# Low parts of the feed-forward halves on VectorE alone, the second norm's weights multiplied in by GpSimd along the rows, turned rows copied out of PSUM by ScalarE

## The reference, cut to what matters

```python
x = x + mix.astype(x.dtype) @ w_out
y, conv_new = _conv_ffn(_rmsnorm(x, norm2), conv_st, w_g, w_u, conv_w, conv_b, w_d)
x = x + y
# _rmsnorm(x, g) = x * rsqrt(mean(x*x) + EPS) * g, over the 1024 columns of a row
# _conv_ffn: g = h @ w_g; u = h @ w_u; (gelu(causal dwconv3(g)) * u) @ w_d, with 2816 inner columns
```

## Time and profile before

| | |
|---|---|
| median of 3 runs | 1403.74 us |
| profiled execution | 1402.94 us, of which span 1401.1 us |
| TensorE busy | 1362.7 us, 97% of the span |
| VectorE, ScalarE, GpSimd busy | 55%, 34%, 39% of the span |
| chain that ended last | TensorE 91% |
| mean granted clock of TensorE | 0.992 |

### The profile page before, as it was taken

One profiled execution on the slowest core, in us unless ns is written; L12 is line 12 of the kernel. 1 busy time (PEld: TensorE's weight loads), 2 busy tenths in 40 slices (PEclk: granted clock), 3 DMA queues, 4 the chain that ended last, 5 costly groups with the idle time before them and its releaser, 6 DMA issues.

```text
span 1401.1 us, 23239 instructions
## 1 busy us (share of the span) xinstructions
PE 1362.7 (97%) x9267; PEld 1235.9 (88%) x9267; DVE 774.9 (55%) x1394; ACT 472.3 (34%) x970; POOL 539.7 (39%) x503
## 2 busy tenths in 40 slices
PE   7999999999999999979999999999999999999997
PEld 6988888889998788879999999999999878888886
DVE  4544131557642455788666666667666676333335
ACT  5341242333332244654333333333333351120212
POOL 5130342457642344684444434344444261120200
PEclk9999999999999999989999999999999999999999
DMA  6222632344427675111212122121212671130203
GB/s 244 72 81 83 214 117 80 106 154 148 132 77 260 235 232 175 68 67 48 94 58 85 59 84 80 62 95 57 86 57 85 225 284 64 64 128 19 110 15 120
DMA packets 81754, 158.56 MB, mean 113 GB/s; under 512 B 6967, under 2 KB 42579, under 8 KB 81135
## 3 DMA queue, kind: packets, MB, share of 16 engines
q1 hardware_dynamic: 81503, 157.01, 32.4%
q10 hardware_dynamic: 144, 0.07, 0.0%
HBM read 110.71 MB, written 46.34 MB: 112 GB/s over the span
## 4 chain that ended last, share of the span: by engine, by line
PE 91%; DVE 3%; POOL 2%; DMA 1%; ACT 1%; issue 1%; SPq 0%; DVEq 0%; ACTq 0%; POOLq 0%
PE bank L93 17%; PE bank L95 16%; PE bank L94 16%; PE bank L110 11%; PE bank L111 11%; PE bank L112 11%; PE bank L2029 1%; PE bank L1222 1%; PE bank L1279 1%; PE bank L1982 1%; DMA m_t_in<-scratch_pT 1%; PE bank L1297 1%; PE bank L2012 0%; PE bank L2041 0%; DMA p_arena<-in_x 0%
## 5 line engine op out<-in xcount | busy, mean ns | idle before, releaser
L303 POOL TENSOR_TENSOR w_lo<-w_raw,w_hi 128x512 fp32r<-128x512 f32 x75 | 106.1, 1429 | 154.6 <-ACT w_hi L298 154.6
L2742 DVE TENSOR_TENSOR d_x<-bank,d_x 128x512 f32<-128x512 f32 x126 | 85.5, 689 | 139.9 <-PE bank L95 139.8
L927 POOL TENSOR_TENSOR w_lo<-w_raw,w_hi 128x1024 fp32r<-128x1024 f32 x33 | 79.1, 2409 | 132.7 <-ACT w_hi L1004 132.5
L110 PE MATMUL bank<-f_t_hi,w_hi 128*128 128x256 f32 (+1 forms) x412 | 121.9, 296 | 0.0
L111 PE MATMUL bank<-f_t_lo,w_hi 128*128 128x256 f32 (+1 forms) x412 | 121.6, 295 | 0.0
L112 PE MATMUL bank<-f_t_hi,w_lo 128*128 128x256 f32 (+1 forms) x412 | 121.5, 295 | 0.0
L93 PE MATMUL bank<-w_hi,p_h1T_hi 128*128 128x512 f32 x288 | 113.0, 392 | 1.0 <-POOL w_lo L927 1.0
L93 PE MATMUL bank<-w_hi,d_a_hi 128*128 128x512 f32 x288 | 113.7, 395 | 0.0
L94 PE MATMUL bank<-w_lo,d_a_hi 128*128 128x512 f32 x288 | 113.7, 395 | 0.0
L95 PE MATMUL bank<-w_hi,d_a_lo 128*128 128x512 f32 x288 | 113.6, 395 | 0.0
L110 PE MATMUL bank<-f_b_hi,w_hi 128*128 128x320 f32 (+1 forms) x360 | 108.3, 301 | 4.3 <-DVE f_gate_prompt L2481 3.6
(11 more groups left out here) (326 smaller groups left out, 3644.5 us busy)
## 6 DMA issues: line engine op xcount, KB each, us to landing
w_raw<-in_w SPq DMA_DIRECT2D x81, 512.0 KB, 4.7
e_a_lo<-scratch_act SPq DMA_DIRECT2D x22, 576.0 KB, 7.1
scratch_pN<-p_n_out SPq DMA_DIRECT2D x36, 256.0 KB, 2.1
c_lo<-in_w SPq DMA_DIRECT2D x16, 512.0 KB, 6.4
scratch_act<-c_hi SPq DMA_DIRECT2D x22, 320.0 KB, 2.1
scratch_pT<-p_t_out SPq DMA_DIRECT2D x36, 192.0 KB, 1.9
scratch_act<-c_lo SPq DMA_DIRECT2D x22, 256.0 KB, 2.0
p_arena<-in_x SPq DMA_DIRECT2D x9, 512.0 KB, 6.0
```

Source lines behind the costliest of these rows:

```text
L110: pe.matmul(out, stat[0], mov[0], start=start, stop=False, skip_group_check=True)
L303: pool.tensor_tensor(lo, self.unit_source(n), hi.bitcast(F32), ALU.subtract).then_inc(self.unit_split, 1)
L927: pool.tensor_tensor(w_lo[:, i % NS_, :], raw[:, i % 2, :], w_hi[:, i % NS_, :].bitcast(F32), ALU.subtract).then_inc(g["piece_split"], 1)
L2742: dve.tensor_tensor(x, bank[DOWN_BANKS[n % 8]], x, ALU.add).then_inc(added.sem, 1)
```

## The change

Three things move, and the hand-written order with them.

1. The weights `norm2` are no longer multiplied in after the turn. GpSimd multiplies each row tile by them before, along the rows (`apply_gain`, new name `("gained", c)` in the order, one 128x1024 operation for each of nine tiles, between `sum` and `scaled`). For that the 1024 weights must lie in every partition: SyncE first copies the column form to a row in DRAM (1024 elements of 4 bytes) and later loads this row into all partitions (`gain`, 512 KB). `scaled` now waits for `gained`.
2. The turned rows are copied out of PSUM by ScalarE (`raw_rows` with ACTIVATE Copy), two 128x512 copies for each tile. Tile 7's copies (`last_rows`) move to ScalarE's program in gate_up.
3. All fourteen low parts of the row operands are made by VectorE, in ScalarE's order of high parts. VectorE's program at the start of gate_up is rewritten for that; GpSimd keeps the low parts of the weights alone.

```diff
+    def apply_gain(self, pool, c):
+        self.gain_in.wait(pool, 32)
+        pool.wait_ge(self.x_loaded[c], 32)
+        pool.tensor_tensor(self.x9[:, c, :], self.x9[:, c, :], self.gain[:, :], ALU.mult).then_inc(self.gained, 1)
+
+    def raw_rows(self, act, bank, c, i):
         p, at = (0, c) if c < 5 else (1, c - 5)
         dst = (self.k1, self.k2)[i][p][:, :, at * P:(at + 1) * P]
-        gain = self.cols[:, K_N2 + i * KH:K_N2 + (i + 1) * KH].unsqueeze(2).to_broadcast([P, KH, P])
-        return dve.tensor_tensor(dst, bank.rearrange("p (k f) -> p k f", k=KH), gain, ALU.mult)
+        return act.activation(dst, bank.rearrange("p (k f) -> p k f", k=KH), ACT.Copy)
...
-        order += {4: [("scaled", 0)], 5: [("scaled", 1)], 6: [("scaled", 2), ("unit", 0)],
-                  7: [("plus", 0), ("plus", 1), ("unit", 1), ("scaled", 3)], 8: [("t", 0, 0)]}.get(s, [])
+        order += {4: [("gained", 0), ("scaled", 0)], 5: [("gained", 1), ("scaled", 1)], 6: [("gained", 2), ("scaled", 2), ("unit", 0)],
+                  7: [("plus", 0), ("plus", 1), ("unit", 1), ("gained", 3), ("scaled", 3)], 8: [("t", 0, 0)]}.get(s, [])
...
         def scale(act, c):
             act.wait_ge(g["norm_root"], M_STEPS.index(c) + 1)
-            act.wait_ge(x_loaded[c], 32)
+            act.wait_ge(half.gained, TURNED.index(c) + 1)
             act.activation(x9[:, c, :], x9[:, c, :], ACT.Copy, scale=rstd2[:, c:c + 1]).then_inc(half.scaled, 1)
...
         load_piece(1)
+        sp.dma_start(row.rearrange("o (k p) -> p (o k)", p=P), a["cols"][:, K_N2:K_N2 + KD],
+                     allow_slow_non_contiguous=True).then_inc(half.gain_in.sem, 16)
...
             elif x[0] == "sum" and x[2] == 1:
+                if x[1] == 1:
+                    sp.wait_ge(g["state_out"], 16)
+                    half.gain_in.wait(sp, 16)
+                    sp.dma_start(half.gain[:, :], row.to_broadcast([P, D])).then_inc(half.gain_in.sem, 16)
...
-        for x in ((1, 0), (1, 1), (0, 5)):
-            half.lo(pool, x)
         done.hidden(pool)
         done.states(pool)
         pool.memset(gp[:, 0:2], 0.0).then_inc(zeroed, 1)
-        half.lo(pool, (1, 4))
-        half.unit_lo(pool, 7)
-        half.unit_lo(pool, 8)
-        half.lo(pool, (1, 5))
-        for n in range(9, 7 * NF):
+        for n in range(7, 7 * NF):
             half.unit_lo(pool, n)
...
+        half.lo(dve, (0, 2))
         half.lo(dve, (0, 3))
         take_up1(0)
         half.lo(dve, (0, 4))
-        last_rows()
-        for k in range(3):
-            half.turned_sum(dve, 1, k)
+        half.lo(dve, (1, 0))
+        half.lo(dve, (1, 1))
         for t in range(QUADS):
             f, p = divmod(t, 2)
             if t != 1:
                 take_c22(t)
             if t == 0:
+                half.lo(dve, (0, 5))
                 half.lo(dve, (0, 6))
+                for k in range(3):
+                    half.turned_sum(dve, 1, k)
                 half.lo(dve, (1, 2))
-                half.turned_sum(dve, 1, 3)
-                half.lo(dve, (1, 3))
...
             take_c21(t)
+            if t == 0:
+                half.lo(dve, (1, 3))
+                half.turned_sum(dve, 1, 3)
+                half.lo(dve, (1, 4))
+                take_up1(1)
+                half.lo(dve, (1, 5))
+                half.lo(dve, (1, 6))
+                take_c22(1)
             conv(t)
```

More of the change, by code:

```diff
@@ L383, in half_split @@
     def half_split(self, x):
-        return (self.half_pool, HALF_POOL.index(x) + 1) if x in HALF_POOL else (self.half_dve, HALF_DVE.index(x) + 1)
+        return self.half_dve, HALF_DVE.index(x) + 1
     def halves_wait(self, eng, p):
-        for order, s in ((HALF_POOL, self.half_pool), (HALF_DVE, self.half_dve)):
-            eng.wait_ge(s, max(i for i, x in enumerate(order) if x[0] == p) + 1)
+        eng.wait_ge(self.half_dve, max(i for i, x in enumerate(HALF_DVE) if x[0] == p) + 1)
     def hi(self, act, x):
@@ L430, in build @@
         res = nc.dram_tensor("scratch_res", (RT, P, D), F32, kind="Internal").ap()
+        row = nc.dram_tensor("scratch_row", (1, D), F32, kind="Internal").ap()
         act_a = nc.dram_tensor("scratch_act", (NF, P, ROWS), F32, kind="Internal").ap()
@@ L438, in build @@
         done = back(nc, a, o, mem_m, early, half, done, const[:, :], cols, col_m, col_d, ssq, ssn, rstd2, power, w, raw, bank,
-                    sem, block)
+                    row, sem, block)
         tiles = DownTiles(a, mem_d, mem_e, w, plain, act_a, old)
@@ L1661, in back_entries @@
         elif x[0] == "turn_n":
-            out += [(x + (i,), "dve") for i in range(2)]
+            out += [(x + (i,), "act") for i in range(2)]
         elif x[0] in ("num", "um"):
@@ L1665, in back_entries, with back @@
     return out
-def back(nc, a, o, mem, early, half, done, ident, cols, col_m, col_d, ssq, ssn, rstd2, power, w, raw, bank, sem, block):
+def back(nc, a, o, mem, early, half, done, ident, cols, col_m, col_d, ssq, ssn, rstd2, power, w, raw, bank, row, sem, block):
     order = back_order()
@@ L1876, in _ @@
                     .then_inc(g["piece_split"], 1)
+            elif name == "gained":
+                half.apply_gain(pool, s)
             elif name == "unit":
                 half.unit_lo(pool, s)
-            elif name == "lo" and x[1:] in HALF_POOL:
-                half.lo(pool, x[1:])
     @block.scalar
@@ L1935, in _ @@
                 Done.scale(act, s)
+            elif name == "turn_n":
+                if s == TURNED[0]:
+                    act.wait_ge(g["state_out"], 16)
+                if s == TURNED[5]:
+                    Done.raw_free(act)
+                for i in range(2):
+                    wait_filled(act, x + (i,))
+                    half.raw_rows(act, ring.bank(x + (i,)), s, i).then_inc(taken["act"], 1)
             elif name == "unit":
@@ L2153, in _ @@
                 clear_state()
-            elif name == "turn_n":
-                if s == TURNED[0]:
-                    dve.wait_ge(g["state_out"], 16)
-                if s == TURNED[5]:
-                    Done.raw_free(dve)
-                for i in range(2):
-                    wait_filled(dve, x + (i,))
-                    u = half.raw_rows(dve, ring.bank(x + (i,)), s, i)
-                    u.then_inc(taken["dve"], 1)
             elif name == "plus":
@@ L2166, in _ @@
                 half.turned_sum(dve, s, x[2])
-            elif name == "lo" and x[1:] in HALF_DVE:
+            elif name == "lo":
                 half.lo(dve, x[1:])
@@ L2346, in units, with last_rows @@
                 half.unit_hi(act, n)
+        def last_rows():
+            act.wait_ge(turned, 1)
+            for s in range(2):
+                u = half.raw_rows(act, bank[TURN_BANKS[s]], LATE, s)
+            u.then_inc(half.raw_done, 1)
         done.scale(act, LATE)
@@ L2352, in _ @@
         half.hi(act, (1, 1))
+        last_rows()
         copy_u2(0)
@@ L2356, in _ @@
         half.hi(act, (0, 6))
-        half.hi(act, (1, 4))
         copy_p1(1)
+        units(7, 8)
         half.hi(act, (1, 2))
         half.hi(act, (1, 3))
-        units(7, 8)
+        half.hi(act, (1, 4))
         half.hi(act, (1, 5))
@@ L2446, in _ @@
     def _(dve):
-        def last_rows():
-            dve.wait_ge(turned, 1)
-            for s in range(2):
-                u = half.raw_rows(dve, bank[TURN_BANKS[s]], LATE, s)
-            u.then_inc(half.raw_done, 1)
         def take_up1(t):
@@ L2550, in _ @@
             take_c21(t)
+            if t == 0:
[6 more added lines that the diff above has]
+                take_c22(1)
             conv(t)
             if t == 0:
-                take_up1(1)
-                half.lo(dve, (1, 6))
-                take_c22(1)
                 half.plus(dve, 1, 0)
```

38 lines of the change are left out of this document (19 added, 19 removed).

## The result

The change makes the kernel slower: 1427.91 us, the median of 4 runs (1425.49 to 1428.45), against 1403.62 for the kernel before beside it; the ratio is 1.0164, with a 95% interval of 1.0149 to 1.0178. The direction was predicted, the size was not: +24.3 us where +11.5 were forecast, and above the range's end of 1423. The profiled execution spans 1425.7 us (before 1401.1), at a mean granted clock of 0.983 (before 0.992).

What follows compares the result with a forecast made beforehand. TensorE, 97% busy, was taken to bound the kernel, with 16 to 17 us to win in one passage. Terms 2.8+4.5+4.7-1.3+0+2.6-1.8 gave +11.5 us on 1402.9, hence a 1415 us median, own range 1409 to 1421, stated range 1404 to 1423.

Steps and rivals of the forecast that it cites:

- Step 2: Back block, tile 3: its multiplication on GpSimd comes behind weight unit 1's low part, so turn 3 is later, +4.5 us.
- Step 3: Tile 4: its multiplication waits behind turn 3's copies and units 2 and 3; +4.7 us, +5.7 if the clock falls.
- 6: First product: its PSUM bank is cleared by ScalarE behind squares, a high part and other copies; +2.6 us.
- Step 5: Turn 6: multiplications of tiles 5 and 6 replace GpSimd's low part of 4.20, the wait of 3.48 stays; 0 (±1.5).
- Step 4: The last `m_mix_b_lo`: of TensorE's 2.06 us wait 0.8 is left; -1.3 us (between -2.1 and +1).
- The price's upper end: GpSimd's 128x1024 multiplication: priced at 2.39 us, with 3.28 beside a busy VectorE kept as upper end.
- Step 7: First quads of gate_up: the wait before (0,5) and its low clock go, waits before (1,2) and (1,4) come; -1.8 us.
- a rival: The clock falls again behind the three last new waits, up to three times 3 us; 1421 to 1424 us, chance 0.17.
- Step 1: Back block, tiles 0 to 2: GpSimd multiplies tile 0 only behind a root, turn 0 later by +2.8 us; others 0.
- That the passage runs through: Rival: VectorE keeps ahead of TensorE, all 10.7 us of waits and both low-clock stretches go; 1399 us, chance 0.10.
- The row of weights: Rival: its 4-byte elements or load block SyncE's queue and turn 0 waits for a landing; about 1418 us, chance 0.04.

Runs made afterwards that it cites:

- e6: The change with ScalarE's squares for row tile 6 moved in front of `scaled` 5; 1426.5 us, ratio 1.0145.
- e9: The change with each of GpSimd's nine multiplications cut to the first 512 of 1024 columns; 1418.9 us, ratio 1.0101.
- e10: The change with unread transposes filling TensorE's waits before turn 0 and product (43,5); 1426.1 us, ratio 1.0150.
- e5: The change with unread transposes before turns 0, 3, 4 and 6 and products (1,2) and (21,5); 1431.0 us, ratio 1.0190.
- e3: The change with the nine multiplications moved ahead in GpSimd's program; 1413.3 us, ratio 1.0060.
- e8: The kernel before with unread transposes in front of turn 6 and products (0,5) and (21,5); 1408.5 us, ratio 1.0012.
- e11: Low parts on VectorE alone, its copies of tiles 5 and 6 ahead, tile 7's copies by ScalarE, weight unit 7's high part later; 1399.8 us, ratio 0.9962.
- e1: The change with parts 1 and 2 undone, leaving only the low parts on VectorE; 1403.5 us, ratio 0.9993.
- e2: The change without the multiplications by norm2 and their row loads; 1399.5 us, ratio 0.9965.

## Why the prediction was wrong

*The forecast* held in direction, at turn 0, in Steps 2 and 3 to within 0.9 us, and in 6: turn 0 waits 2.68 (2.8 predicted), turn 3 4.82 (4.5), the first product 2.08 (2.6). ScalarE's copies take 0.6 and less, the multiplication alone 2.36 (2.39).

*Step 5 failed.* It said that the multiplications of tiles 5 and 6 only take the place of the low part of 4.20 us that goes, "0 (±1.5)". Turn 6 lost 3.2 us more. I had seen the four links, but not added them as one chain of 12.6 us, and had priced two multiplications at 4.8 where they took 7.2. e6 shows the chain (turn 6 2.0 us earlier when one link is cut), e9 its length (from turn 5 to turn 6 4.7 us at half the length, where 7.7 were taken).

*Step 4 failed.* It gave 1.3 us back because "after step 3 everything but TensorE has had time". GpSimd had not: it was the engine that was late, with two low parts of 2.5 us and the multiplication of tile 5 to do, and turn 5, which the prediction doesn't name, became a new wait of 1.57. Turn 5 came 2.8 us later against turn 4, not 1.3 earlier. VectorE waited 12.90 us for `m_mix_b_hi`, which stands in ScalarE's queue behind `scaled` of tile 8, and that waited for GpSimd's multiplication until 599.94; so the mixer's rows of this step reached GpSimd late too, ahead of tile 5's weights. TensorE's speed plays no part: from turn 4 to turn 5 it is 21.1 us in the change, in e6 and in e10, and 21.2 in e5, where the clock is up; at half the length it is 18.5 (e9), before 18.2. In e3, with tile 5's multiplication a place earlier, turn 5 isn't waited for.

*The price's upper end was too low.* 3.28 was kept for a multiplication beside a busy VectorE; tiles 5 and 6 took 3.64 and 3.59. The other seven took 2.36 to 2.85.

*The low clock was put in the wrong places.* Step 7 took 3.0 us off for it, and a rival added 3 us for each new wait in the passage, which would have given 1421 to 1424. e5 refutes the rival's price: 1.4 us for the whole passage, most of it behind turn 0, where dense work follows (1.2 at turn 1: most of Step 1's error in the table). For the 3.0 of Step 7 no run shows as much: with the low clock behind (0,5) filled away the kernel before gained nothing (e8), though that count is not clean. The rival came nearer to the time than the forecast, for a reason that didn't hold. Behind (43,5), which the prediction never looked at since the change doesn't touch it, the fall cost 2.4 in this execution, and as it comes and goes from profile to profile no run shows that to be the change's.

*Step 7* came within 1.0 us in sum (-0.8 for -1.8), but not by its parts. The wait before (0,5) is gone. That before (1,2) is 4.11 for 2.8, because the first sum took 2.32 beside GpSimd's low part of weight unit 7 (1.1 of the difference; e11 moves that part away). That before (1,4) is 0.24 for 3.0, because TensorE came later at a granted clock of 0.50 (654 to 660 us), 1.2 GHz; with the clock up it is 2.49 (e5).

*The other rivals.* That the passage runs through needed a wait under 1 us before turn 6: it was 6.61. The row of weights was never waited for by TensorE in the change, and GpSimd's first multiplication starts at 541.04, where the root ends.

*The small excess of Steps 2 and 3* can be read from the rows. Of Step 2's 0.9 us, 0.5 is the multiplication at tile 3 (2.85 for 2.39, beside VectorE's sums of weights); 0.3 was there at turn 2 already, where the forecast had nothing. Step 3's 0.6 is the low clock behind turn 3, which the prediction had priced as an alternative (+5.7): with the clock up the step is 4.5 (e5), with it low 5.3 and 5.4 (the change, e10).

What stays open: why the clock falls behind some waits and not behind others of the same length.

## What to carry to other kernels

Before work goes to an engine that is idle on average, follow one item through all the queues it will pass, and where two items share the queues, add both passes as one chain, at the durations that the engine shows beside its neighbour there: that chain, not the sum of busy time, is the price. Count a low TensorE clock only behind waits that have dense TensorE work after them; where another engine sets the next start, it is paid already. And cut a change into its parts: two of the three here cost nothing by themselves (e1, e2), and the low parts on VectorE, with the weights left where they were and VectorE's copies moved ahead, beat both kernels by a little (e7: 0.23% under the kernel before).
